# Value stage of a PEER layer: 768 gathered columns in place of 896, two rounded banks in place of one, and dense slots in the memory of used weights

## The reference, cut to what matters

```python
ue = jnp.take(u, eid, axis=0)
act = jax.nn.gelu(jnp.einsum('thkd,td->thk', ue, xt), approximate=False)
ve = jnp.take(v, eid, axis=0)
return jnp.einsum('thk,thkd->td', gate * act, ve)
```

## Time and profile before

| | |
|---|---|
| median of 3 runs | 2986.62 us (2985.75 to 2989.51) |
| profiled execution, its own time | 2987.69 us |
| its span in the profile | 2985.9 us |
| granted clock of TensorE, mean | 0.880 |
| busy: TensorE, VectorE, ScalarE, GpSimd | 78%, 67%, 38%, 31% |
| value stage, chunk 0 to the last product | about 2478 to 2962 us |

### The profile page before, as it was taken

The page is one execution under the profiler, slowest core; times in us unless marked ns, Lnnn a source line. Parts: engine busy times, 40 slices in busy tenths (PEclk is TensorE's granted clock), DMA queues, the critical chain, the costliest instruction groups (busy, mean ns, idle before and its releaser), DMA issues.

```text
span 2985.9 us, 28929 instructions
## 1 busy us (share of the span) xinstructions
PE 2328.2 (78%) x10371; PEld 1847.9 (62%) x10371; DVE 1999.5 (67%) x2386; ACT 1129.0 (38%) x1262; POOL 922.4 (31%) x773
## 2 busy tenths in 40 slices
PE   8999999999999999899999990000022249999996
PEld 7888888888888888688888780000011146665664
DVE  5456555555444565745665659999999897777777
ACT  5444344444444554444344342221322243222222
POOL 1000000000000000000000017888887877767774
PEclk9999999999999999999999995555555569999998
DMA  7666556566666546455556449999999967999996
GB/s 272 208 187 194 168 177 189 185 194 185 189 185 188 157 134 205 160 174 168 169 183 232 155 164 409 419 416 415 407 421 410 420 273 306 407 406 390 408 408 272
DMA packets 165303, 792.12 MB, mean 265 GB/s; under 512 B 20188, under 2 KB 20240, under 8 KB 131248
## 3 DMA queue, kind: packets, MB, share of 16 engines
q1 hardware_dynamic: 105344, 390.12, 40.2%
q0 software_dynamic: 59824, 400.23, 33.0%
HBM read 788.17 MB, written 2.10 MB: 265 GB/s over the span
## 4 chain that ended last, share of the span: by engine, by line
PE 61%; DVE 17%; DMA 10%; issue 6%; POOL 4%; ACT 1%; POOLq 0%; SPq 0%; DVEq 0%; ACTq 0%
PE banks L713 53%; DVE ring L2122 10%; DMA v_rows<-in_peer_v_rest,eid 7%; DMA ring<-in_peer_u,eid 2%; POOL v_rows L684 2%; PE banks L745 2%; PE banks L1093 1%; POOL ring L633 1%; PE banks L1062 1%; DVE banks L2194 1%; PE banks L1087 1%; POOL w_x L670 1%; DVE onehots L2101 1%; DMA v_raw<-in_peer_v_dense 1%; PE banks L725 1%
## 5 line engine op out<-in xcount | busy, mean ns | idle before, releaser
L713 PE MATMUL banks<-w_split,xT 128*128 128x512 f32 x7008 | 1615.0, 392 | 8.1 <-DVE xT L1529 5.5
L713 PEld LDWEIGHTS banks<-w_split,xT 128*128 128x128 f32 x7008 | 1317.6, 189 | 283.0 <-DVE xT L1529 7.2
L1482 DVE TENSOR_TENSOR w_split<-w_raw,w_split 128x1024 fp32r<-128x1024 f32 x592 | 722.3, 1224 | 745.6 <-ACT w_split L1125 744.6
L1125 ACT ACTIVATE w_split<-w_raw 128x1024 fp32r<-128x1024 f32 x592 | 626.2, 1059 | 914.2 <-PE banks L713 877.8
L2122 DVE CUSTOM_DVE_ANT_0 ring<-ring,banks 128x2048 f32<-128x2048 f32 x193 | 436.4, 2284 | 49.7 <-DMA ring<-in_peer_u,eid 37.1
L2194 DVE SCALAR_TENSOR_TENSOR banks<-v_rows,wgt,banks 128x896 f32<-128x896 f32 x254 | 293.0, 1154 | 81.6 <-DMA v_rows<-in_peer_v_rest,eid 76.6
L567 POOL DMA_DIRECT2D row_a<-in_final_g x1 | 0.5, 534 | 1068.9 <-DVE ao L1744 1068.9
L633 POOL DMA_INDIRECT ring<-in_peer_u,eid x256 | 243.0, 949 | 257.1 <-DVE eid L2054 174.0
L1093 PE MATMUL banks<-v_raw,wT 128*128 128x512 f32 (+1 forms) x1024 | 301.3, 437 | 0.7 <-ACT wT L1393 0.7
L641 POOL TENSOR_TENSOR ring<-ring,h 128x2048 f32<-128x2048 f32 x63 | 284.7, 4519 | 39.4 <-DMA ring<-in_peer_u,eid 39.1
L1062 PE MATMUL banks<-onehots 128*128 128x128 f32 x512 | 103.0, 367 | 243.0 <-DVE onehots L2101 231.7
(11 more groups left out here) (313 smaller groups left out, 1356.3 us busy)
## 6 DMA issues: line engine op xcount, KB each, us to landing
w_raw<-in_a_w_in SPq DMA_DIRECT2D x192, 512.0 KB, 3.5
v_raw<-in_peer_v_dense SPq DMA_DIRECT2D x128, 576.0 KB, 7.9
w_raw<-in_b_w_in SPq DMA_DIRECT2D x128, 512.0 KB, 3.6
w_raw<-in_w_in SPq DMA_DIRECT2D x112, 512.0 KB, 3.5
w_raw<-in_a_w_out SPq DMA_DIRECT2D x64, 512.0 KB, 3.8
w_raw<-in_b_w_out SPq DMA_DIRECT2D x32, 512.0 KB, 4.1
w_raw<-in_w_out SPq DMA_DIRECT2D x32, 512.0 KB, 4.6
w_raw<-in_peer_wq SPq DMA_DIRECT2D x32, 512.0 KB, 3.7
```

The lines of the kernel that those rows point to most:

```text
L713: last = mm(ps[half][:, 2 * t + n, :], xt[:, xp, kk, tok], w_split[:, s, wp, n * BANK:(n + 1) * BANK], start=(k == 0 and xp == 0 and wp == ...
L1125: fn(w_split[:, k % SPLIT_SLOTS, 0, :], w_raw[:, k % RAW_SLOTS, :], ACT.Copy).then_inc(hi_done, 1)
L1482: v.tensor_tensor(w_split[:, s, 1, :], w_raw[:, k % RAW_SLOTS, :], w_split[:, s, 0, :].bitcast(F32), ALU.subtract).then_inc(split_done, 1)
```

## The change

768 columns are gathered and 1280 are dense. Of the dense ones 1024 (two banks) go through the rounded passes and 256 are plain; `rounded` now issues a matmul for each of the two banks. `v_raw`, `v_split`, `v_rows` and the operations on them change their widths with it, on ScalarE (L1448), VectorE (L2202, L2194, and the additions to `h`) and TensorE.

The dense slots are placed anew. Three lie in `RAW`, and two more at 8 KB behind the starts of `T1` and `T2`, in the part of `wT` that chunks 16 to 25 use; they come into use from chunk `V_FROM` = 30. `raw_slot` gives slot, number of its load and the chunk that must be done before it: three slots in turn for chunks 0 to 29, five after. SyncE's loop is written out into 128 loads. The second slot of `w_x` moves to the memory of the lists, and the last two slots of `v_rows` to the end of `ROWS`.

```diff
--- before.py
+++ after.py
@@ -64,12 +64,15 @@
 GROUP_HEADS = 2
 TILE_GROUPS = PEER_HEADS // GROUP_HEADS
 GROUP_PICKS = GROUP_HEADS * TOPK
-V_GATHERED = 896
+V_GATHERED = 768
 V_DENSE = D - V_GATHERED
-V_SPLIT = BANK
+V_SPLIT = 2 * BANK
+V_ROUNDED = V_SPLIT // BANK
 V_PLAIN = tuple((lo, min(BANK, V_DENSE - lo)) for lo in range(V_SPLIT, V_DENSE, BANK))
-V_BANKS = 1 + len(V_PLAIN)
-V_CHUNKS = 4
+V_BANKS = V_ROUNDED + len(V_PLAIN)
+V_CHUNKS = 3
+V_MORE = 2
+V_FROM = 30
 V_SLOTS = 6
 V_EARLY = 4
 SCATTER = 4
@@ -99,6 +102,16 @@
 
 DOTS = sum(not by_pool(r) for r in range(TILES * PICKS))
 SUMS = TILES * PICKS - DOTS
+
+
+def raw_slot(c):
+
+    if c < V_FROM:
+        return c % V_CHUNKS, c // V_CHUNKS + 1, c - V_CHUNKS
+    s, n = (c - V_FROM) % (V_CHUNKS + V_MORE), (c - V_FROM) // (V_CHUNKS + V_MORE)
+    if s < V_CHUNKS:
+        return s, V_FROM // V_CHUNKS + n + 1, c - V_CHUNKS - (V_MORE if n else 0)
+    return s, n + 1, c - V_CHUNKS - V_MORE
 
 
 def one_hot_row(m):
@@ -349,12 +362,12 @@
         early_rows = packer(ROWS, LISTS)
         late = packer(SCR + 32 * KB, 16 * KB + 512)
         v_split = [late(f"v_split{n}", [P, 2, V_SPLIT], F32R) for n in range(2)]
-        v_raw = ([early_raw(f"v_raw{n}", [P, V_DENSE]) for n in range(V_CHUNKS - 1)]
-                 + [late(f"v_raw{V_CHUNKS - 1}", [P, V_DENSE])])
+        v_raw = ([early_raw(f"v_raw{n}", [P, V_DENSE]) for n in range(V_CHUNKS)]
+                 + [sb(f"v_raw{V_CHUNKS + n}", [P, V_DENSE], F32, start + 8 * KB) for n, start in enumerate((T1, T2))])
         v_rows = ([early_rows(f"v_rows{n}", [P, V_GATHERED]) for n in range(V_EARLY)]
-                  + [late(f"v_rows{V_EARLY}", [P, V_GATHERED]),
-                     sb(f"v_rows{V_EARLY + 1}", [P, V_GATHERED], F32, ROWS + 24 * KB - V_ROW)])
-        w_x = [sb("w_x0", [P, 2, TILES, P], F32R, MASKS), early_raw("w_x1", [P, 2, TILES, P], F32R)]
+                  + [sb(f"v_rows{n}", [P, V_GATHERED], F32, ROWS + 24 * KB - (V_SLOTS - n) * V_ROW)
+                     for n in range(V_EARLY, V_SLOTS)])
+        w_x = [sb("w_x0", [P, 2, TILES, P], F32R, MASKS), early_rows("w_x1", [P, 2, TILES, P], F32R)]
         row_g2 = sb("row_g2", [P, D], F32, T1)
         row_b2 = sb("row_b2", [P, D], F32, T2)
 
@@ -451,7 +464,7 @@
         weighed_by_act = sem("weighed_by_act")
         scattered = sem("scattered")
         w_stored = sem("w_stored")
-        v_raw_landed = [sem(f"v_raw_landed{s}") for s in range(V_CHUNKS)]
+        v_raw_landed = [sem(f"v_raw_landed{s}") for s in range(V_CHUNKS + V_MORE)]
         v_products = sem("v_products")
         v_landed = [sem(f"v_landed{n}") for n in range(V_SLOTS)]
         v_used = sem("v_used")
@@ -537,20 +550,16 @@
             load_pairs(w_out_2[0], "mix_out", 0, 1)
             load_pairs(peer_wq_2[0], "peer_q", 0, 1)
 
-            def load_v(c, s):
-
-                if not isinstance(c, int):
-                    sp.wait_ge(v_products, c + (1 - V_CHUNKS))
-                elif s + 1 == V_CHUNKS:
-                    sp.wait_ge(scattered, TOKENS // SCATTER + 2)
-                sp.dma_start(v_raw[s][:, :], peer_v_dense[0, bass.ds(c * N_KEYS, N_KEYS), :]).then_inc(v_raw_landed[s], 16)
+            def load_v(c):
+
+                s, _, before_it = raw_slot(c)
+                if before_it >= 0:
+                    sp.wait_ge(v_products, before_it + 1)
+                sp.dma_start(v_raw[s][:, :], peer_v_dense[0, c * N_KEYS:(c + 1) * N_KEYS, :]).then_inc(v_raw_landed[s], 16)
 
             sp.wait_ge(keys_known, TILES)
-            for s in range(V_CHUNKS):
-                load_v(s, s)
-            with sp.Fori(1, N_KEYS // V_CHUNKS) as i:
-                for s in range(V_CHUNKS):
-                    load_v(i * V_CHUNKS + s, s)
+            for c in range(N_KEYS):
+                load_v(c)
             for n in range(2 * TILES):
                 t, b = divmod(n, 2)
                 cols_ = slice(b * COLS, (b + 1) * COLS)
@@ -1080,17 +1089,20 @@
 
             def multiply_v(c):
 
-                s, u = c % V_CHUNKS, c % 2
+                u = c % 2
+                s, nth, _ = raw_slot(c)
                 first, last = c == 0, c + 1 == N_KEYS
 
                 def rounded(t, wp, vp):
-                    return mm(v_banks[t][0], w_x[u][:, wp, 1 - t, :], v_split[u][:, vp, :],
-                              start=first and wp + vp == 0, stop=last and vp == 1)
-
-                pe.wait_ge(v_raw_landed[s], 16 * (c // V_CHUNKS + 1))
+                    for n in range(V_ROUNDED):
+                        ins = mm(v_banks[t][n], w_x[u][:, wp, 1 - t, :], v_split[u][:, vp, n * BANK:(n + 1) * BANK],
+                                 start=first and wp + vp == 0, stop=last and vp == 1)
+                    return ins
+
+                pe.wait_ge(v_raw_landed[s], 16 * nth)
                 for t in range(TILES):
                     for n, (lo, width) in enumerate(V_PLAIN):
-                        mm(v_banks[t][1 + n][:, 0:width], wT[:, 1 - t, c, :], v_raw[s][:, lo:lo + width],
+                        mm(v_banks[t][V_ROUNDED + n][:, 0:width], wT[:, 1 - t, c, :], v_raw[s][:, lo:lo + width],
                            start=first, stop=last)
                 pe.wait_ge(w_hi, c + 1)
                 pe.wait_ge(v_hi, c + 1)
@@ -1444,8 +1456,9 @@
                 if c >= 2:
                     act.wait_ge(v_products, c - 1)
                 fn(w_x[u][:, 0, :, :], wT[:, :, c, :], ACT.Copy).then_inc(w_hi, 1)
-                act.wait_ge(v_raw_landed[c % V_CHUNKS], 16 * (c // V_CHUNKS + 1))
-                fn(v_split[u][:, 0, :], v_raw[c % V_CHUNKS][:, 0:V_SPLIT], ACT.Copy).then_inc(v_hi, 1)
+                s, nth, _ = raw_slot(c)
+                act.wait_ge(v_raw_landed[s], 16 * nth)
+                fn(v_split[u][:, 0, :], v_raw[s][:, 0:V_SPLIT], ACT.Copy).then_inc(v_hi, 1)
 
             def keep_sum(t):
 
@@ -2199,7 +2212,7 @@
 
                 u = c % 2
                 dve.wait_ge(v_hi, c + 1)
-                v.tensor_tensor(v_split[u][:, 1, :], v_raw[c % V_CHUNKS][:, 0:V_SPLIT],
+                v.tensor_tensor(v_split[u][:, 1, :], v_raw[raw_slot(c)[0]][:, 0:V_SPLIT],
                                 v_split[u][:, 0, :].bitcast(F32), ALU.subtract).then_inc(v_lo, 1)
 
             for m in range(SCATTERS, TILES * SCATTERS):
```

## The result

The changed kernel takes 3006.56 us (median of 5 runs, 3001.58 to 3012.41) against 2987.54 (5 runs, 2985.75 to 2991.26): 1.0061 of the time before, 95% interval 1.0045 to 1.0077. It is slower, as forecast, by 19 us and not by 45; 3006.56 lies inside the wide range of 2990 to 3062, and outside the forecast's own case of 3014 to 3048. The profiled execution took 3003.42 us with a span of 3001.7, 15.8 more than before.

A forecast was written before the change was run, and what follows sets the result against it. GpSimd, held by VectorE's longer subtraction, was taken as the bound: 126 chunks x 4.05 = 510.3 us and 12 of stalls put the last products at 3007.5 against 2962.5, +45, so 3032 us. Range 2990 to 3062.

The forecast's parts named there:

- the forecast's own case: Value stage: GpSimd sets the pace at 3.90 to 4.17 us a chunk, giving 3014 to 3048 us; chance 0.66.
- TensorE, 3.63 a chunk: Value-stage matmuls: 3.63 us a chunk after, 0.08 more, which matters only if TensorE sets the pace.
- Transfers: Value-stage loads and gathers: 1.442 MB a chunk at 409 GB/s, 3.53 us, 0.16 less than before; they leave the path.
- VectorE, ScalarE: Value stage: VectorE's subtraction 1.22 us, additions 1.02 each, 3.4 at most a chunk; ScalarE's rounding 1.06, hidden.
- GpSimd, "I take 4.05": GpSimd's cycle in the value stage: 3.11 us of work plus a gather held 0.93 by VectorE's subtraction, about 4.05.
- Slots, "at no cost": Three dense slots for chunks 3 to 29: 12.3 us round, 4.1 a chunk; no cost, or 1 us if landing stays 7.9.
- Stalls, 12 us: GpSimd's two idle times (2 x 3.2 us), shorter ones (about 2) and the gain and bias loads: 12 us in full.
- Start, 0.5: Ahead of the value stage: three dense preloads 0.2 MB larger while transfers are full, 0.5 us.
- rival 1: Value stage: TensorE sets the pace at 3.63 us a chunk; -5 us, 2982; chance 0.12, with rival on transfers included.
- rival 3: Value stage: waits chain up, values late from three slots, over 4.2 us a chunk; 3054 to 3090; chance 0.11.
- rival 2: Value stage: the exclusion costs, but partly, 3.65 to 3.88 us a chunk; 2990 to 3011; chance 0.11.
- Signs: Value-stage trace: gathers or weight subtractions of 1.7 to 1.9 us, TensorE idle, windows near 355 GB/s, chain through w_x.

The follow-up runs named there:

- e3: Changed kernel, but a dense slot is free once the plain products and the subtraction reading it are done; 2991.5 us, 1.0007 of the kernel before.
- e1: Changed kernel with three dense slots for all 128 chunks, never five; 3057.18 us in one run.
- e2: Changed kernel with five dense slots in use from chunk 12 in place of 30; 2991.62 us, 1.0011 of the kernel before.
- e10: Changed kernel without GpSimd's subtraction of the weights from chunk 2 on (output wrong in the low part); 2990.35 us in one run.
- e4: Changed kernel's slots with the column widths of the kernel before (896 gathered, 512 rounded, 640 plain); 2998.74 us, 1.0041 of the kernel before.
- e7: Kernel of e3 with VectorE's subtraction made as two halves of 512 columns, one ahead of each addition; 2984.86 us, 0.9988 of the kernel before.
- e5: Kernel of e3 with the second bank's second and third rounded pass left out in all chunks but the last (output wrong); 2972.33 us in one run.
- e6: Kernel of e3 without GpSimd's subtraction of the weights from chunk 2 on (output wrong in the low part); 2976.00 us in one run.

## Why the prediction was right in sign and wrong in size

The forecast's +45 us came wholly from a GpSimd cycle of 4.05 us, which the changed kernel comes near in only four chunks from 34 on (64 to 67, 3.93 to 4.03); the loss that was measured came from the dense slots, which the forecast had put at nothing. So that the kernel is slower came out right, but in good part by luck.

- **TensorE, 3.63 a chunk**: right to the hundredth; it is the pace of chunks 34 to 56 and 70 to 120.
- **Transfers**: right as a rate, for chunks from 34 on: 397 GB/s are enough for 3.63 and the queues reached 402 in the fast window, and the stretches of 3.87 of the earlier trace rows are gone. In the first quarter the landing of each single load is on the path, through the slots.
- **VectorE, ScalarE**: 1.02 and 1.23 us measured, 1.02 and 1.22 forecast; 1.05 for 1.06.
- **GpSimd, "I take 4.05"**: this step failed. It held that VectorE's subtraction waits for whatever GpSimd runs, its subtraction or a gather, and then holds the next gather for 0.79 to 0.93. The rows that I had read, show it waiting for a second gather, behind which the weight subtraction stands; behind a first gather it starts at once. The trace of before had this already: its 62 subtractions that start in a gather with no L670 right behind it all take 0.68 or 0.69 us. With that, a gather is held by 0.50 and not by 0.79 to 0.93, and 3.11 + 0.50 = 3.61 is reachable, under the floor of 3.74 that I had given; the cycle settles at TensorE's 3.63. The cycle of 3.90 to 4.05 is real (e3, 3.95) but isn't the only stable one, and the changed kernel was in the other from chunk 34 on, but for those four chunks. 126 x 4.05 = 510 us became 490.95 for 127 chunks, 3.87 on the mean.
- **Slots, "at no cost"**: failed. The round was written as 12.3 us in three chunks, 4.1 each, and thought to be hidden behind 4.05; it is four chunks long, goes through GpSimd, and took 17.08 us in the chain, 4.27 each. e1, e2 and e3 show that it makes the loss, e10 that about half of it (8.2 of 17.7) is the slots' own. e4 puts the slots alone, with the widths of before, at 10.5.
- **Stalls, 12 us**: chunks 57, 58, 64 to 69 and 121 were 14.6 us over 3.63 in sum. The sum is near, its parts are not: the two idle times cost 5.9 (forecast: 6.4, and 2 for shorter ones that cost nothing here), the chunks at the two loads 8.7 (forecast: 4.2).
- **Start, 0.5**: 2.3 in this pair of profiles; the starts of all profiles lie between 2476.2 and 2482.1, so this stays open.
- **Rivals**: the outcome is a mixture that I hadn't listed: rival 1's pace for three quarters of the chunks, and a round through the slots for the first quarter, which rival 3 named ("values late from three slots", "over 4.2") but for all chunks. The time lies in rival 2's 2990 to 3011, but its cost of 3.65 to 3.88 in each chunk is the pace of no stretch of the changed kernel; and by the forecast's own sum 3.65 a chunk gives 3032 - 126 x 0.40 = 2982, not 2990. Rival 1 alone might have been a small gain: e7, with the release of the slots and the length of a meeting mended, is at 0.9988.
- **Signs**: those that I had named did show, in the first quarter: 345 GB/s, gathers of 1.74, TensorE waiting for `w_x`. There they belong to the round through the slots as well, so they couldn't tell the two apart; TensorE's full busy time from chunk 34 on could.

The Trainium skill, page "SBUF — State Buffer", section "SBUF: two separate sides", says that of a VectorE instruction with two SBUF inputs and a GpSimd instruction that reads SBUF, whichever starts first holds the shared port pair for its whole length. For GpSimd's weight subtraction the traces agree (1.43 to 1.52). For gathers they agree one way only: a gather that starts behind VectorE's subtraction is held (1.45, 1.74), while 99 subtractions that started in a running gather took 1.22 or 1.23 and weren't. Why those wait that start more than 0.30 us into a gather with L679 right behind it isn't shown.

## What to carry to other kernels

When two engines exclude each other, don't take the worst meeting as the cycle: list for each pair of instructions who waits for whom, and look for every phase that repeats itself, since a kernel can sit in a cheap one or a dear one and shift at a stall. Count over the whole trace how often an instruction waits in each kind of meeting before a rule is made of one row. When a buffer loses a slot, follow the round of one slot through every queue until it comes back, with the waits for other engines in it, and ask whether the slot could be given back by its last reader and not by the end of the chunk: here that was worth 15 us for one semaphore more.

## What the runs showed of the hardware

- A fp32 subtraction with both inputs in SBUF on VectorE and an indirect gather issued by GpSimd: a gather that starts while the subtraction runs is held: it ends 0.95 us after the subtraction's recorded end less 0.13; the subtraction isn't held by a running gather (99 of 99), except in those that are followed at once by an elementwise operation on GpSimd. In these it is free if it starts up to 0.30 us into the gather (latest: 0.29 in the changed kernel, 0.30 in e7), and held to the gather's end if it starts later (earliest: 0.32 and 0.34).
- The two queues brought 407 GB/s in e5 (2500 to 2600 us) with loads of 5,120 bytes a row and gathers of 3,072 a row, about as much as the 409 with 4,608 and 3,584 before.
- Around chunks 57 and 121 GpSimd has an idle time of some 3 us: 3.33 twice before, 3.03 and 3.14 in e5 with no releaser in the profile; 2.68 and 2.77 in the changed kernel, put down there to VectorE's addition, as is e3's 2.76 at chunk 121. What makes them isn't known. They cost 3.8 and 2.2 us in the changed kernel and nothing in e6, which has slack on GpSimd.
